# Differential attention on one core: a shift per half of the second map, the turns spread over the score halves, the copies split two and two in another way

## The reference

```python
scale = 1.0 / math.sqrt(DIFF_QK)                      # DIFF_QK = 32
def block(args):                                      # 128 queries at a time
    qb, bi = args
    qpos = bi * BLOCK + jnp.arange(BLOCK, dtype=jnp.int32)
    bias = table[:, t5_bucket(kpos[None, :] - qpos[:, None])]
    sc = jnp.einsum('bqhmd,bkhmd->bmhqk', qb, k).astype(jnp.float32) * scale + bias[None, None]
    p = jax.nn.softmax(sc, axis=-1)
    a = p[:, 0] - lam * p[:, 1]
    return jnp.einsum('bhqk,bkhd->bqhd', a.astype(v.dtype), v)
```

## Time and profile before

| | us |
|---|---|
| median of 3 runs | 4045.36 (4042.28 to 4050.85) |
| the profiled execution | 4044.97 |
| its span, first to last instruction | 4043.2 |
| granted TensorE clock, mean | 0.982 of full speed |
| differential stage of layer 0 | about 1184.9 to 1693.2 |

### The profile page before, as it was taken

The page is one execution under the profiler, slowest core; times in us unless marked ns, Lnnn a source line. Parts: engine busy times, 40 slices in busy tenths (PEclk is TensorE's granted clock), DMA queues, the critical chain, the costliest instruction groups (busy, mean ns, idle before and its releaser), DMA issues. The chain is left out here.

```text
span 4043.2 us, 51539 instructions
## 1 busy us (share of the span) xinstructions
PE 3793.2 (94%) x19002; PEld 2624.1 (65%) x19002; DVE 2236.1 (55%) x3973; ACT 1658.7 (41%) x2886; POOL 2286.1 (57%) x1381
## 2 busy tenths in 40 slices
PE   8999999999989999889989999999999899998898
PEld 8789774555546666557777897755555466665577
DVE  3003125555569999875531030255556699998755
ACT  3102103333348888760031021033333488887610
POOL 1221325877768888744512213267777688886455
PEclk9999999999999999999989999999999999999999
DMA  5433445233420222245354334422233202223353
GB/s 176 126 132 118 145 134 123 62 82 71 91 59 1 57 57 58 57 112 190 130 174 130 128 120 140 144 68 55 66 73 77 59 1 57 57 58 72 109 177 135
DMA packets 180864, 392.43 MB, mean 97 GB/s; under 512 B 18014, under 2 KB 100168, under 8 KB 168968
## 3 DMA queue, kind: packets, MB, share of 16 engines
q1 hardware_dynamic: 179752, 387.75, 34.3%
q10 hardware_dynamic: 864, 1.41, 0.2%
HBM read 255.93 MB, written 135.67 MB: 97 GB/s over the span
## 5 line engine op out<-in xcount | busy, mean ns | idle before, releaser
L1297 POOL TENSOR_TENSOR mla_sum_pool<-mla_sum_pool,mla_probs 128x1024 f32<-128x1024 f32 (+1 forms) x336 | 777.8, 2315 | 209.0 <-ACT mla_probs L1258 184.2
L1315 DVE TENSOR_REDUCE carry_row_max<-psum 128x1 f32<-128x512 f32 x688 | 474.2, 689 | 416.1 <-PE psum L1130 411.2
L1258 ACT ACTIVATE mla_probs<-psum 128x1024 f32<-128x1024 f32 x384 | 373.3, 1021 | 694.4 <-PE psum L1167 689.7
L1690 DVE TENSOR_REDUCE diff_row_max<-psum 128x1 f32<-128x1024 f32 x512 | 613.4, 1217 | 49.6 <-PE psum L1534 38.9
L1613 ACT ACTIVATE diff_probs<-psum,diff_shift 128x1024 f32<-128x1024 f32 x512 | 566.1, 1111 | 178.0 <-DVE diff_shift L1697 171.8
L1560 PE MATMUL psum<-ident,diff_probs 128*128 128x128 f32 x2048 | 328.1, 284 | 93.0 <-DVE diff_turned L1724 80.9
L638 PE MATMUL psum<-in_x_hi,in_w_hi 128*128 128x512 f32 x1024 | 409.4, 400 | 2.7 <-ACT in_mla_val L745 2.7
L638 PE MATMUL psum<-in_x_hi,in_w_lo 128*128 128x512 f32 x1024 | 405.5, 396 | 0.0
L638 PE MATMUL psum<-carry_firsts,in_w_hi 128*128 128x512 f32 x1024 | 404.5, 395 | 0.0
L1560 PEld LDWEIGHTS psum<-ident,diff_probs 128*128 128x128 f32 x2048 | 215.9, 141 | 265.0 <-issue 254.3
L1671 POOL TENSOR_TENSOR diff_probs<-diff_probs 128x1024 f32<-128x1024 f32 x128 | 305.8, 2389 | 141.6 <-ACT diff_probs L1621 141.3
(11 more groups left out here) (213 smaller groups left out, 7363.7 us busy)
## 6 DMA issues: line engine op xcount, KB each, us to landing
in_w_raw<-in_w_in SPq DMA_DIRECT2D x64, 512.0 KB, 3.9
split_d<-in_out SPq DMA_DIRECT2D x64, 512.0 KB, 2.7
raw_d<-in_out SPq DMA_DIRECT2D x32, 512.0 KB, 2.7
mq_d<-in_out SPq DMA_DIRECT2D x48, 256.0 KB, 3.6
mk_d<-in_out SPq DMA_DIRECT2D x48, 256.0 KB, 4.0
carry_firsts<-split_d SPq DMA_DIRECT2D x48, 256.0 KB, 8.1
carry_weights<-split_d SPq DMA_DIRECT2D x48, 256.0 KB, 7.7
carry_weights<-split_d SPq DMA_DIRECT2D x16, 768.0 KB, 18.1
```

The source lines that it names most:

```text
L1258: nc.scalar.activation(probs[:, s % RING, :].rearrange("p (a n) -> p a n", n=CH), psum[:, S0 + 2 * (s % 2):S0 + 2 * (s % 2) + 2, :], ACT.E ...
L1297: nc.gpsimd.tensor_tensor(acc, start, probs[:, s % RING, mine], ALU.add).then_inc(pool_added, 1)
L1315: nc.vector.tensor_reduce(row_max[:, u % 2, qb, n:n + 1], psum[:, sweep_bank(g), :], AX.X, ALU.max).then_inc(maxed, 1)
L1690: nc.vector.tensor_reduce(row_max[:, n % 2, m, half:half + 1], banks(n, m, half), AX.XY, ALU.max).then_inc(maxed, 1)
```

## The change

Four things, all in the stage above except the first:

1. The scale 1/sqrt(32) is applied to q when the input projection writes it (L834 and L953, eight tiles in all), so the exponentials need no scale. The constants that held its inverse become 1.
2. Second map: each half's exponential uses that half's own negated maximum (`part_shift`) as its bias, and is issued on its own. A small activation, `parts(n)`, then gives for each half exp(own maximum - maximum of the map). `ratios` multiplies the second map's two row sums by it (`weighed`), a further small instruction computes total x lambda (`first_lam`), and the ratio becomes two numbers, one per half. Shift(n,1), a minimum of two numbers, is issued one maximum later, in the round of unit n+1.
3. TensorE's round holds one batch of turns between score halves: scores(0,0), turns 1 of n-3, scores(0,1), products, turns 2, scores(1,0), turns 3, products, turns 0 of n-2, scores(1,1).
4. ScalarE copies batches 1 and 2, VectorE 0 and 3. ScalarE's scaling of 512 columns stands behind the exponential of half (1,0), and in VectorE's round the ratios come ahead of its two copies.

```diff
-            return (act_copied if c % 2 else dve_copied), 2 * n + c // 2 + 1
+            return (act_copied, 2 * n + c) if c in (1, 2) else (dve_copied, 2 * n + (c == 3) + 1)
...
                     if on:
                         scores(n, 0, 0)
-                    turns(n - LAG - 1, 3)
+                    turns(n - LAG - 1, 1)
                     if on:
                         scores(n, 0, 1)
                     products(n, 0)
+                    turns(n - LAG - 1, 2)
+                    if on:
+                        scores(n, 1, 0)
+                    turns(n - LAG - 1, 3)
+                    products(n, 1)
                     turns(n - LAG, 0)
                     if on:
-                        scores(n, 1, 0)
-                    turns(n - LAG, 1)
-                    if on:
                         scores(n, 1, 1)
-                    products(n, 1)
-                    turns(n - LAG, 2)
...
+                    else:
+                        act.wait_ge(maxed, 4 * n + 2 + half + 1)
+                        bias = part_shift[:, n % 2, half:half + 1]
...
+                def parts(n):
+                    act.wait_ge(shifted, 2 * n + 2)
+                    nc.scalar.activation(part[:, n % DEEP1, :], part_shift[:, n % 2, :], ACT.Exp,
+                                         bias=shift[:, n % 2, 1:2], scale=-1.0).then_inc(parted, 1)
...
-                    copy(n - LAG - 1, 3)
                     if on:
-                        exp(n, 0)
-                    if n == UNITS:
-                        scale(n - 1)
-                    copy(n - LAG, 1)
-                    if 1 <= n < UNITS:
-                        scale(n - 1)
+                        exp(n, 0, 0)
+                        exp(n, 0, 1)
                     if n % 2:
                         odd_half((n - 5) // 2)
                     if on:
-                        exp(n, 1)
+                        exp(n, 1, 0)
+                    if 1 <= n <= UNITS:
+                        scale(n - 1)
+                    copy(n - LAG, 1)
+                    if on:
+                        exp(n, 1, 1)
+                        parts(n)
+                    copy(n - LAG, 2)
...
                     dve.wait_ge(exped, 4 * (n + 1))
+                    dve.wait_ge(parted, n + 1)
+                    nc.vector.tensor_tensor(row_sum[:, n % 2, 1, :], row_sum[:, n % 2, 1, :], part[:, n % DEEP1, :],
+                                            ALU.mult).then_inc(weighed, 1)
+                    dve.wait_ge(weighed, n + 1)
...
+                    nc.vector.tensor_scalar(first_lam[:, n % 2:n % 2 + 1], totals[:, 0, qb, h:h + 1], dots[:, 0:1], None,
+                                            ALU.mult).then_inc(lam_ready, 1)
...
-                    copy(n - LAG - 1, 2)
                     if on:
                         maximum(n, 0, 0)
+                    if 1 <= n <= UNITS:
+                        to_shift(n - 1, 1)
+                    if on:
                         maximum(n, 0, 1)
                         to_shift(n, 0)
                     if n == UNITS:
                         mix(n - 2)
-                        ratios(n - 1)
-                        copy(n - LAG, 0)
+                    ratios(n - 1)
+                    if n == UNITS:
                         mix(n - 1)
-                    else:
-                        copy(n - LAG, 0)
-                        ratios(n - 1)
+                    copy(n - LAG - 1, 3)
                     if on:
                         maximum(n, 1, 0)
+                    copy(n - LAG, 0)
+                    if on:
                         maximum(n, 1, 1)
-                        to_shift(n, 1)
                     if n % 2:
                         output((n - 5) // 2)
```

More of the change, by code:

```diff
@@ L833, in _ @@
                         else:
[L834 removed]
+                            nc.scalar.activation(out[:, s, :].bitcast(F32R), tile_banks(g), ACT.Copy, scale=tile_scale(t)
+                                                 ).then_inc(tile_out, 1)
             @block.vector
@@ L1602, in _, with exp @@
             def _(act):
-                def exp(n, m):
-                    act.wait_ge(shifted, 2 * n + m + 1)
-                    if m == 0 and n >= DEEP:
-                        act.wait_ge(turn_done, 4 * (n - DEEP + 1))
-                    if m == 1 and n >= DEEP1:
-                        act.wait_ge(mixed, 2 * (n - DEEP1 + 1))
+                def exp(n, m, half):
+                    if m == 0:
+                        act.wait_ge(shifted, 2 * n + 1)
+                        bias = shift[:, n % 2, 0:1]
+                        if n >= DEEP:
+                            act.wait_ge(turn_done, 4 * (n - DEEP + 1))
+                    else:
+                        act.wait_ge(maxed, 4 * n + 2 + half + 1)
+                        bias = part_shift[:, n % 2, half:half + 1]
+                        if n >= DEEP1:
+                            act.wait_ge(mixed, 2 * (n - DEEP1 + 1))
@@ L1609, in exp @@
                     dst = probs[:, n % DEEP, :] if m == 0 else probs1[:, n % DEEP1, :]
[L1610 removed]
+                    if n >= 2:
                         act.wait_ge(summed, n - 1)
[L1612 to L1615 removed]
+                    nc.scalar.activation(dst[:, half * HALF:(half + 1) * HALF].rearrange("p (a n) -> p a n", n=CH),
+                                         banks(n, m, half), ACT.Exp, bias=bias,
+                                         accum_out=row_sum[:, n % 2, m, half:half + 1]).then_inc(exped, 1)
```

97 lines of the change are left out of this document (54 added, 43 removed).

## The result

The changed kernel takes **4181.65 us** (median of 4 runs, 4178.0 to 4190.79), the kernel before 4047.28 in the same comparison: a ratio of **1.0336**, 95% interval 1.0315 to 1.0358. It is slower by 134 us. The forecast was 4000 us, 3975 to 4038. The profiled execution has a span of 4177.3 us.

The account below looks back on a forecast made before the run. Differential attention was taken as bound by loops of TensorE's transpose batches and VectorE's copies through one bank. Units falling from 7.746 to 7.35 us win 49 us, drain adds 4: 4045.36 - 45 gives 4000 us, range 3975 to 4038.

Parts of the forecast that it names:

- A shift per half: Second map's exponentials start after their own half's maximum; the added small instructions make VectorE pay 0.17 us a unit.
- the chain from the product to the copy: VectorE's small instructions from weighed to its copy, taken as 0.85 us a unit.
- VectorE's bare unit: VectorE's own work per unit of differential attention without waits: 7.15 us after the change, 6.98 before.
- The walk: One unit of the new order stepped through with all waits: slow 7.32, fast 7.20, mean 7.26 us; 0.09 added gives 7.35.
- Slow and fast units: A head's units, 7.915 and 7.575 us by which score half holds the band; forecast within 0.2 of each other afterwards.
- The drain: Two more batches of turns left after each attention layer's last scores: 2 us a layer, +4 us.
- GpSimd's work is unchanged: GpSimd waits longer for ScalarE's scaling, but its additions still end in time: cost 0.
- A: Only slow units gain, to 7.35 us; fast ones stay at 7.575: 4014 us, chance 0.20.
- B: VectorE is full, every instruction costing its whole duration, so no unit gets shorter: 4051 us, chance 0.08.
- C: ScalarE holds exp(1,1) behind copy1, making units 8.0 us: slower, 4081 us, chance 0.10.

Follow-up runs that it names:

- e2: Kernel before plus one unused VectorE product of 128x2 with two SBUF inputs per unit, at the head of the ratio chain: 4109.95 us, ratio 1.0156.
- e4: Control: kernel before plus two unused one-input, one-column (128x1) VectorE instructions per unit at the head of the ratio chain: 4067.87 us, ratio 1.0053.
- e3: Kernel before plus one unused VectorE tensor_scalar of 128x2 with one SBUF input per unit, at the head of the ratio chain: 4111.87 us, ratio 1.0161.
- e1: Changed kernel with the weighing product and the ratio rewritten in one-input, one-column forms, two more instructions a unit: 4035.01 us, ratio to before 0.9974.
- e7: e1 with VectorE computing one factor a unit and ScalarE making the two ratios in one small activation: 3996.34 us, ratio to before 0.9873.

## Why the prediction was wrong

**The step that failed** is the price of the added small instructions, in "A shift per half": "The two VectorE instructions are bounded by 0.13 (an independent one, like shift before copy) and 0.20 (a dependent one)". Its neighbours in the trace were all of one form, one tensor input and one column, or a reduction. Neither weighed (two inputs from SBUF) nor the new ratio (two columns; I priced it as the old one) has that form. Where they run free the price was right: the product's successor starts 0.18 us after it (1448.18 to 1448.36), the copy 0.20 after the ratio (1441.89 to 1442.09), where I had 0.18 and 0.19. But they last 0.60 and 1.22 us on average, 2.35 and 1.87 at most, instead of 0.15 and 0.29, and the sum has no term for waiting on GpSimd. The bound was taken from the nearest size, not from the nearest form.

The term of the sum that this spoils is the chain from the product to the copy, 0.85 us. In layer 0 of the changed kernel it measures 1.07 to 3.40 us, 2.41 on average over units 2 to 61. Put in place of 0.85 it makes VectorE's bare unit 7.15 - 0.85 + 2.41 = 8.71 us; the clock shows 8.724. VectorE is now the bound, and nearly the whole error lies in this term.

**The trace of before had a row that said so**, and I did not list it. VectorE mixes half of each of the last two units itself, with two inputs from SBUF (L1731), beside GpSimd's additions:

```profile
1677.97 2.36 POOL L1671 TENSOR_TENSOR diff_probs<-diff_probs 128x1024 f32<-128x1024 f32 x1 [1.10 <-ACT diff_probs L1621]
...
1679.27 2.14 DVE L1731 SCALAR_TENSOR_TENSOR diff_probs<-diff_probs,diff_ratio 128x1024 f32<-128x1024 f32 x1
...
1682.77 1.27 DVE L1731 SCALAR_TENSOR_TENSOR diff_probs<-diff_probs,diff_ratio 128x1024 f32<-128x1024 f32 x1
1682.93 3.33 POOL L1671 TENSOR_TENSOR diff_probs<-diff_probs 128x1024 f32<-128x1024 f32 x1
```

The same instruction lasts 2.14 us when GpSimd's addition, 1677.97 to 1680.33, is running at its start, and 1.27 when it starts first; then the addition beside it takes 3.33 instead of 2.36. So each holds the other, and it stood in four instructions of 3973. When both start almost together the rows don't say who yields: in the changed kernel a mix starts at 1736.89 and lasts 1.26, though GpSimd's addition is recorded from 1736.71, and the addition then takes 3.65; a product at 1308.19 lasts 0.15 beside a scaling recorded from 1308.18.

The Trainium skill states the exclusion too: SBUF — State Buffer, section "Who interferes with whom", has a VectorE instruction with two SBUF inputs, or one in a mode that uses both read ports, wait for a GpSimd instruction that started first, and the other way round, "not throttle" but fully. By that rule the sum needed a term for waiting on GpSimd. The traces here agree: e2 (two inputs) is held and e4 (one input, one column) is free. That e3 (two columns) is held fits the rule if it ran in such a mode, which no run shows by itself. The rule of the Trainium skill that the prediction did weigh, that each VectorE instruction empties its pipe first, explains none of the loss: in e1 an independent instruction starts 0.12 us after one that lasts 0.20.

**Everything else in the sum, once the two are repaired**, came out close. The walk had 7.26 and took 7.35 us a unit; e7 has 7.287. Slow and fast units have become alike, as forecast. That the predicted 4000 is nearly e7's 3996 is partly luck: e7 is not the change that was predicted. The nearer test is e1, which keeps the change's work on VectorE, and it is at 7.608 us and 4035. Its chain from the weighing to the copy, 0.85 in my sum, is 1.35: seven instructions instead of five, those with two per-partition scalar operands 0.27 long. 7.15 + 0.50 is 7.65 for the measured 7.608. So without any holding, but with two instructions more, the unit is still 0.26 us above the forecast 7.35.

**The drain**: from the ratio of unit 63 to the end of the last output there were 11.4 us before (1681.72 to 1693.16) and 15.5 after (1740.98 to 1756.45), 4 us a layer where I took 2. Together 8 of the 134 us.

**GpSimd**: "GpSimd's work is unchanged" held, its cost of 0 did not. It is what held VectorE. The prediction asked whether GpSimd would be late and not what it does to others.

**The rivals.** A missed. B had the right engine, VectorE full, for a wrong reason: an independent instruction costs less than its duration, as the 0.12 from 1435.04 to 1435.16 in e1 shows. C (ScalarE behind copy1) is refuted by e1 and e7, which keep that order and gain. The slower outcome had a chance of 0.10 by a mechanism that no run shows; the one that the runs show had none.

**What stays open**: who yields when a GpSimd and a VectorE instruction start within some 0.2 us of each other, and why two columns are held where one is not. No run took GpSimd's work away; that GpSimd is what holds rests on the ends that coincide and on the forms that are free.

## What to carry to other kernels

Price a small added instruction by its form (how many inputs from SBUF, how many columns) and by who else is running, not by its size: search the trace for any instruction of that form and look at the spread of its durations, not the mean. Where GpSimd is busy most of the time, keep VectorE's small elementwise instructions at one SBUF input and one column, or give them to ScalarE. A change of two parts can lose in each part and win with both, so repair the whole before rejecting an order.

## What the runs showed of the hardware

- A VectorE tensor_scalar over 128x2 numbers with one SBUF input is held by GpSimd's elementwise instructions, up to 1.80 us in e3; over 128x1 it is not (137 to 146 ns in 256 of them, e4).
- VectorE's reductions over 128x4 numbers from SBUF stay at 158 to 161 ns in the changed kernel, beside the same GpSimd work; ScalarE's 128x2 activation stays at 281 to 316.
- In the kernel before a GpSimd addition beside a VectorE mix with two SBUF inputs takes 3.33 us instead of 2.36, the mix 2.14 instead of 1.27 when the addition came first.
- An independent small VectorE instruction starts 0.08 to 0.12 us after the one before it (1435.65 to 1435.73, 1435.04 to 1435.16 in e1), a dependent one 0.18 to 0.31 (1435.16 to 1435.34, 1435.34 to 1435.65).
